# A long convolution's second stage on quarters of TensorE's array, its swapped spectra made there, and the filter's sine arguments on VectorE

## The chip, the cores and the metric

One Trainium2 chip; the program runs on one of its cores. The metric is the device time of one execution in microseconds (us), the median of several. A core has TensorE (matrix products), VectorE, ScalarE, GpSimd, SyncE (which here only issues transfers), and 16 DMA engines that all queues share. TensorE reads SBUF and writes PSUM, which has eight banks of 128 partitions by 512 fp32 values; VectorE and ScalarE read PSUM.

## The reference, cut to what matters

A backbone of two layers over 1024 latent and 256 context tokens of width 1024. Layer 0 is a Hyena mixer (long convolutions with filters made by a small network with sines), layer 1 is latent attention, each followed by a gated feed-forward part. The change touches layer 0's filters and convolutions:

```python
def hyena_filters(L, fw1, fb1, fw2, fb2, fw3, freq):
    ...
    hdn = jnp.sin(freq[0] * (feats @ fw1 + fb1))
    hdn = jnp.sin(freq[1] * (hdn @ fw2 + fb2))
    h = (hdn @ fw3).reshape(L, HY_ORDER, 2, D_MODEL)
    ...
def bidir_long_conv(z, h_fwd, h_bwd, bias):
    L = z.shape[1]
    k = jnp.concatenate([h_fwd, jnp.zeros_like(h_fwd[:1]), h_bwd[1:][::-1]], axis=0)
    kf = jnp.fft.rfft(k.astype(jnp.float32), n=2 * L, axis=0)
    zf = jnp.fft.rfft(z.astype(jnp.float32), n=2 * L, axis=1)
    y = jnp.fft.irfft(zf * kf, n=2 * L, axis=1)[:, :L]
    return (y + z.astype(jnp.float32) * bias).astype(z.dtype)
...
    z = v
    for n, gate in enumerate((x1, x2)):
        z = gate * bidir_long_conv(z, filt[:, n, 0], filt[:, n, 1], fbias[n])
```

## The kernel before

**The filter's sines.** Five products with fw1 and ScalarE (arguments) give 64 x 2560 arguments in turns, in fa. To bring them into half a turn on each side, four elementwise operations run on GpSimd: add MAGIC, subtract it (which rounds), subtract the result, clamp; a semaphore (s_fc) stands between each two. ScalarE takes the sine, TensorE the second layer (128 x 2560), and the four operations run on GpSimd again, after it has issued six loads for VectorE's modulation vectors. Meanwhile VectorE reduces weight tiles against the conditioning (first_mods, 18 tiles, two reductions each, by a custom operation), then scales the eight x tiles and splits them into high and low parts (Hs0), which TensorE's first weight stream waits for tile by tile. SyncE waits for the second reduction (s_fr) before it loads the convolution's constants, and behind them the next weight tiles of that stream.

**The convolution** is a Fourier transform in two stages of matrix products, all in fp32. STEPS is an order of steps written out by hand, and each engine walks it. There are five rounds (it): four for 256 channels each of the latent tokens, and one for the context; in each two convolutions (o). The steps:

- K: filter values (h2 by fw3), decay on VectorE, first stage, eviction to s1 by ScalarE, a store to t2k by GpSimd's queue that regroups the partitions. Six s1 slots.
- Z: signal transposed, first stage in two halves, s1, stores to t2z.
- S: second stage of the filter: t2k by st gives the spectrum, 64 real and 64 imaginary rows, which ScalarE copies to kk[:, 0]. SyncE then copies the two halves of the partitions crosswise into kk[:, 1] by eight DMAs, so that a product with the real spectrum can meet both parts.
- M: eight units. Each has two products of t2z with st (banks 4, 5 in turn), VectorE's multiplication by kk[:, 0] and kk[:, 1] into prod (128 x 1024), and four products with mi and mib (real and crossed part) accumulated in banks 6, 7. ScalarE evicts to one of three w1 slots, GpSimd's queue stores to t2w. TensorE issues unit u's signal products before unit u-1's inverse products.
- B: waits for all t2w stores, then 32 small products with f1i, and VectorE's gating.

The order inside a round is M(it,0), S(it,1), B(it,0), K(it+1,0), Z(it,1), K(it+1,1), M(it,1), Z(it+1,0), S(it+1,0), B(it,1). GpSimd's queue issues the stores in that order, and ScalarE evicts in it.

## Time and profile before

| | before |
|---|---|
| median of 3 runs | 3764.3 us (3762.15 to 3768.49) |
| the profiled execution | 3763.62 us |
| its span, first to last instruction | 3761.9 us |
| TensorE, VectorE, ScalarE, GpSimd busy | 91%, 59%, 35%, 10% |
| mean granted TensorE clock | 0.969 |
| until TensorE's first weight stream runs on | 0 to about 112 us |
| convolution | about 441 to 1162 us |
| a middle round of it | 140 us (841 to 981) |

Times of one instruction come from one profiled execution. In the records a fp32 product appears as two pairs of a weight load (LDWEIGHTS, engine PEld) and a multiply (MATMUL, engine PE), so x2 is one product. A product's duration is modelled and includes its way through the array; what TensorE spends on it is the distance from one start to the next. Idle time of an engine is put down to what ended it.

### The profile page before, as it was taken

To read this page: it belongs to the slowest core of one execution; us is meant where nothing else is said; L and a number is where in the kernel's file an instruction comes from. 1 tells how busy PE (TensorE), PEld (TensorE's weight loads), DVE (VectorE), ACT (ScalarE), POOL (GpSimd) and SP (SyncE) were. 2 spreads that over 40 slices of the span, in tenths; PEclk is the share of its full clock that TensorE was granted. 3 is DMA by queue.
4 is the path that set the end of the run, shared out by engine and by line. 5 is a ranking of instruction groups with operands and counts; after the bars stand their busy time and mean duration, and the time that the engine had idled before them with its cause. 6 is when DMAs were issued, how large, how long until landed. Compare 5 with 4: busy or idle time off the path is not lost.

```text
span 3761.9 us, 44226 instructions
## 1 busy us (share of the span) xinstructions
PE 3412.2 (91%) x16326; PEld 2710.6 (72%) x16326; DVE 2203.0 (59%) x3232; ACT 1325.8 (35%) x2255; POOL 357.7 (10%) x518
## 2 busy tenths in 40 slices
PE   1999988988989989999989988999999979999897
PEld 0788655565677768888868876777777758888685
DVE  8989832332334565545566755555555676666576
ACT  1212233333333353333334543333333353333344
POOL 5111123323330000000000020000000000000000
PEclk9999999999998999999999999999999989999899
DMA  5655799989763132222353431000000223332632
GB/s 192 207 198 201 201 149 149 155 155 150 167 200 135 56 109 84 81 86 90 137 186 98 163 118 45 8 7 7 7 31 0 73 93 123 104 107 87 235 99 89
DMA packets 191373, 430.87 MB, mean 115 GB/s; under 512 B 34560, under 2 KB 61504, under 8 KB 189512
## 3 DMA queue, kind: packets, MB, share of 16 engines
q1 hardware_dynamic: 138984, 291.65, 24.6%
q0 software_dynamic: 51936, 131.27, 16.1%
q10 hardware_dynamic: 288, 5.77, 0.4%
q8 instruction: 103, 1.69, 0.2%
q14 instruction: 62, 0.50, 0.1%
HBM read 262.50 MB, written 81.00 MB: 91 GB/s over the span
## 4 chain that ended last, share of the span: by engine, by line
PE 71%; DVE 12%; DMA 10%; ACT 3%; issue 2%; POOL 1%; SPq 0%; DVEq 0%; ACTq 0%; POOLq 0%
PE ps L602 18%; PE ps L603 18%; PE ps L604 18%; DMA t2z<-s 3%; DMA t2w<-w 3%; PE ps L2375 2%; PE ps L2350 2%; DMA t2k<-s 2%; PE ps L672 1%; DVE mx L2726 1%; PE ps L2333 1%; PE ps L2233 1%; PE ps L2334 1%; PE ps L2319 1%; PE ps L2301 1%
## 5 line engine op out<-in xcount | busy, mean ns | idle before, releaser
L602 PE MATMUL ps<-HB,gsp 128*128 128x512 f32 x1232 | 487.6, 396 | 38.2 <-DVE HB L778 22.0
L603 PE MATMUL ps<-HB,gsp 128*128 128x512 f32 x1232 | 484.1, 393 | 0.0
L604 PE MATMUL ps<-HB,gsp 128*128 128x512 f32 x1232 | 483.0, 392 | 0.0
L1056 DVE TENSOR_TENSOR gsp<-graw,gsp 128x512 fp32r<-128x512 f32 x330 | 226.4, 690 | 262.7 <-ACT gsp L1035 261.9
L1035 ACT ACTIVATE gsp<-graw 128x512 fp32r<-128x512 f32 x330 | 206.8, 628 | 326.2 <-PE ps L604 266.9
L602 PEld LDWEIGHTS ps<-HB,gsp 128*128 128x128 f32 x1232 | 233.9, 190 | 91.8 <-issue 21.5
L602 PE MATMUL ps<-tsp,wdh 128*128 128x512 f32 x616 | 244.1, 396 | 35.6 <-DVE tsp L1313 35.6
L604 PEld LDWEIGHTS ps<-HB,gsp 128*128 128x128 f32 x1232 | 233.6, 190 | 49.9
L603 PEld LDWEIGHTS ps<-HB,gsp 128*128 128x128 f32 x1232 | 233.9, 190 | 46.1 <-issue 1.0
L602 PE MATMUL ps<-Hs,whi 128*128 128x512 f32 (+1 forms) x576 | 206.1, 358 | 47.3 <-DVE Hs L2532 47.3
L603 PE MATMUL ps<-tsp,wdh 128*128 128x512 f32 x616 | 242.2, 393 | 0.0
L604 PE MATMUL ps<-tsp,wdh 128*128 128x512 f32 x616 | 242.2, 393 | 0.0
L603 PE MATMUL ps<-Hs,whi 128*128 128x512 f32 (+1 forms) x576 | 205.5, 357 | 0.0
L604 PE MATMUL ps<-Hs,wlo 128*128 128x512 f32 (+1 forms) x576 | 204.9, 356 | 0.0
L1289 ACT ACTIVATE wdh<-wd 128x512 fp32r<-128x512 f32 x154 | 97.3, 632 | 249.8 <-PE ps L604 235.1
L2645 DVE TENSOR_TENSOR prod<-ps,kk 128x1024 f32<-128x1024 f32 x80 | 97.6, 1224 | 137.6 <-PE ps L2319 136.5
L2059 ACT ACTIVATE s<-ps 128x512 f32<-128x512 f32 x160 | 94.9, 597 | 226.6 <-PE ps L2233 88.5
L1310 DVE TENSOR_TENSOR wdh<-wd,wdh 128x512 fp32r<-128x512 f32 x154 | 106.1, 689 | 115.9 <-ACT wdh L1289 115.2
L1976 POOL DMA_DIRECT2D R<-residual_scratch x6 | 5.3, 891 | 1719.8 <-DMA hidden_scratch<-R 957.7
L2135 ACT ACTIVATE pts<-ps 128x512 fp32r<-128x512 f32 (+1 forms) x192 | 96.4, 524 | 189.8 <-PE ps L2410 188.9
L602 PEld LDWEIGHTS ps<-tsp,wdh 128*128 128x128 f32 x616 | 117.2, 190 | 63.6 <-issue 33.1
L602 PEld LDWEIGHTS ps<-Hs,whi 128*128 128x128 f32 x576 | 109.6, 190 | 66.9 <-issue 46.3
(263 smaller groups left out, 7941.9 us busy)
## 6 DMA issues: line engine op xcount, KB each, us to landing
graw<-in_w_gu SPq DMA_DIRECT2D x176, 256.0 KB, 2.6
mring<-in_mod_w POOLq DMA_DIRECT2D x78, 512.0 KB, 4.3
hidden_scratch<-R SPq DMA_DIRECT2D x154, 256.0 KB, 2.4
traw<-hidden_scratch SPq DMA_DIRECT2D x154, 256.0 KB, 2.6
t2k<-s POOLq DMA_DIRECT2D x80, 256.0 KB, 10.2
t2z<-s POOLq DMA_DIRECT2D x160, 128.0 KB, 8.9
kk<-kk SPq DMA_DIRECT2D x80, 256.0 KB, 7.3
t2w<-w POOLq DMA_DIRECT2D x160, 128.0 KB, 4.9
```

Source lines behind the costliest of these rows:

```text
L602: pe.matmul(o, wh, xh, start=start, stop=False, skip_group_check=onto)
L603: pe.matmul(o, wh, xl, start=False, stop=False, skip_group_check=onto)
L604: return pe.matmul(o, wl, xh, start=False, stop=stop, skip_group_check=onto)
L1035: act.activation(gsp[U % 3][:, 0, :], graw[:, q, W_SLOT[i], :], ACT.Copy).then_inc(w.hi, 1)
L1056: dve.tensor_tensor(gsp[U % 3][:, 1, :], graw[:, q, W_SLOT[i], :], gsp[U % 3][:, 0, :].bitcast(F32), ALU.subtract).then_inc(w.lo, 1)
L1289: act.activation(wdh[v % 3][:, 0, :], wd[W_SLOT[i]][:, kt, :], ACT.Copy).then_inc(w.hi, 1)
L1310: dve.tensor_tensor(wdh[v % 3][:, 1, :], wd[W_SLOT[i]][:, kt, :], wdh[v % 3][:, 0, :].bitcast(F32), ALU.subtract).then_inc(w.lo, 1)
L2059: act.activation(s1[b % 6][:], bank(BANK_B[b % 2]), ACT.Copy).then_inc(s_be, 1)
L2135: act.activation(dst, src, ACT.Copy).then_inc(s_ma, 1)
L2350: mm = pe.matmul(ps[:, BANK_A[au % 2], 64 * k:64 * k + 64], t2w[:, at:at + P], f1i[:, which, :], start=True, stop=True)
L2375: mm = pe.matmul(bank(use.bank, n), whq[:, k, o:o + P], cq[:, k, t0:t0 + n], start=(k == 0), stop=(k == 2))
L2645: dve.tensor_tensor(prod[zi % 2][:], bank(BANK_C[(n["c"] + u) % 2]).unsqueeze(1).to_broadcast([P, 2, 512]), kk[:, :, 512 * u:512 * (u + 1) ...
```

## The change

1. **Quarters.** st and mi are cut into 64x64 blocks. A full 128x128 product becomes four products (QUARTERS), with row half r of the input and output half c, each on its own quarter of the array; their results go to two banks (one for each r in S and the signal part of M). Input halves and output halves hold different frequencies now: of each pair of frequency groups one lies in the upper and one in the lower partitions, with real and imaginary parts in the two banks.
2. **Swaps.** st2 holds the blocks in the order real, imaginary, imaginary, real, so M's signal part makes spectrum and swapped spectrum by products (v = 0, 1). kk[:, o] holds one unswapped copy per convolution, and SyncE's eight DMAs of each S step are gone. VectorE multiplies both banks by kk, read twice.
3. **Inverse.** Each product with mi or mib is four quarters, with the input halves c and output halves r; results of two units share two banks.
4. **PSUM.** Signal results use banks 4, 5 and 0, 1 in turn (A's), outputs 6, 7 and 2, 3 (B's), so M waits for A and B to be emptied, and the next K or Z for the outputs (EMPTIED_BEFORE).
5. **Sine arguments.** The eight operations move from GpSimd to VectorE: the first four behind the first six modulation tiles, the other four behind the last high-low split of x.

```diff
+    half = [slice(32 * r, 32 * r + 32) for r in range(2)]
+    st2, mi2 = np.zeros((P, NB, 4, 32)), np.zeros((2, 2, 32, 2, NB, 2, 64))
...
@@ sync
-                elif kind == "S":
-                    for q in range(4):
-                        sp.wait_ge(s_ke, n["k"] + 2 * q + 2)
-                        cols_ = slice(1024 * q, 1024 * (q + 1))
-                        sp.dma_start(kk[0:64, 1, cols_], kk[64:P, 0, cols_]).then_inc(s_sw[q], 16)
-                        sp.dma_start(kk[64:P, 1, cols_], kk[0:64, 0, cols_]).then_inc(s_sw[q], 16)
@@ gpsimd
-            for layer, rows in enumerate((64, P)):
-                pool.wait_ge(s_fa, NFC * (layer + 1))
...
-                if layer == 0:
-                    mod_load(3)
+            mod_load(3)
@@ scalar, step S
-                    for u in range(8):
+                    for u in range(4):
                         act.wait_ge(s_kf, n["k"] + u + 1)
-                        act.activation(kk[:, 0, 512 * u:512 * u + 512], bank(BANK_C[(n["c"] + u) % 2]), ACT.Copy
-                                       ).then_inc(s_ke, 1)
+                        act.activation(kk[:, o, 1024 * u:1024 * u + 1024].rearrange("p (a r c) -> p r a c", a=2, r=2),
+                                       pair(SETS_S[u % 2]).rearrange("p r (a c) -> p r a c", a=2), ACT.Copy).then_inc(s_ke, 1)
@@ tensor, step S
+                            for r, c in QUARTERS:
+                                e = 4 * u + 2 * h + c
+                                mm = pe.matmul(ps[rows64(c), SETS_S[u % 2] + r, CW * h:CW * (h + 1)],
+                                               st[rows64(r), const_at(it, e), 0:64],
+                                               t2k[rows64(r), 512 * e + CW * o:512 * e + CW * (o + 1)], start=True, stop=True)
@@ tensor, step M
+                        if u == 1:
+                            pe.wait_ge(s_ae, n["A"])
...
+                            for v in range(2):
+                                for r, c in QUARTERS:
+                                    e = 2 * u + c
+                                    mm = pe.matmul(ps[rows64(c), SETS_C[u % 2] + r, CW * v:CW * (v + 1)],
+                                                   st[rows64(r), const_at(it, e), 64 * v:64 * v + 64],
+                                                   t2z[rows64(r), CW * e:CW * (e + 1)], start=True, stop=True)
...
+                            y = u - 1
+                            pe.wait_ge(s_pr, n["z"] + y + 1)
+                            if y == 2:
+                                pe.wait_ge(s_be, n["B"])
+                            if y in (4, 6):
+                                pe.wait_ge(s_de, n["d"] + y - 2)
+                            for v, m_ in enumerate((mi, mib)):
+                                for r, c in QUARTERS:
+                                    mm = pe.matmul(ps[rows64(r), SETS_D[y // 2 % 2] + c, CW * (y % 2):CW * (y % 2 + 1)],
+                                                   m_[rows64(c), const_at(it, 2 * y + c), 64 * r:64 * r + 64],
+                                                   prod[y % 2][rows64(c), r, CW * v:CW * (v + 1)], start=v == 0, stop=v == 1)
...
@@ vector
+            def reduce_arguments(layer, rows):
+                dve.wait_ge(s_fa, NFC * (layer + 1))
+                x, u = fa[0:rows, :], fu[0:rows, :]
+                dve.tensor_scalar(u, x, MAGIC, None, ALU.add).then_inc(s_fc, 1)
...
+            first_mods(range(6))
+            reduce_arguments(0, 64)
+            first_mods(range(6, 18))
...
+            reduce_arguments(1, P)
@@ vector, step M
-                        dve.tensor_tensor(prod[zi % 2][:],
-                                          bank(BANK_C[(n["c"] + u) % 2]).unsqueeze(1).to_broadcast([P, 2, 512]),
-                                          kk[:, :, 512 * u:512 * (u + 1)], ALU.mult).then_inc(s_pr, 1)
+                        dve.tensor_tensor(prod[zi % 2][:].rearrange("p r (v c) -> p r v c", v=2),
+                                          pair(SETS_C[u % 2]).rearrange("p r (v c) -> p r v c", v=2),
+                                          kk[:, o, 512 * u:512 * (u + 1)].rearrange("p (r c) -> p r c", r=2).unsqueeze(2)
+                                          .to_broadcast([P, 2, 2, CW]), ALU.mult).then_inc(s_pr, 1)
```

TensorE's row in step M, two units of the steady part, before (a row is one product; "waits" names the semaphores; ps is PSUM):

```order
L2319 MATMUL ps<-t2z,st 128x256 [waits products_ready]
L2319 MATMUL ps<-t2z,st 128x256
L2333 MATMUL ps<-prod,mi 128x256 [waits inverse_emptied,products_ready]
L2334 MATMUL ps<-prod,mib 128x256
L2333 MATMUL ps<-prod,mi 128x256
L2334 MATMUL ps<-prod,mib 128x256
L2319 MATMUL ps<-t2z,st 128x256 [waits products_ready]
L2319 MATMUL ps<-t2z,st 128x256
```

And now (x7 and x4 count products in a row):

```order
L2330 MATMUL ps<-t2z,st 64x256 [waits products_ready]
L2330 MATMUL ps<-t2z,st 64x256 x7
L2346 MATMUL ps<-prod,mi 64x256 [waits inverse_emptied,products_ready]
L2346 MATMUL ps<-prod,mi 64x256 x3
L2346 MATMUL ps<-prod,mib 64x256 x4
```

Six full products of a unit have become sixteen quarter products: eight with st behind one another, then four with mi and four with mib.

VectorE's row at the start, behind the first six modulation tiles (macc and modv), now:

```order
L2514 ISA macc 128x1
L2520 TENSOR_TENSOR modv<-macc,modb 128x12 [waits mod_w_used]
L2537 TENSOR_SCALAR fu<-fa 64x2560 [waits filter_arguments_out_or_even_products_used]
L2539 TENSOR_SCALAR fu<-fu 64x2560 [waits filter_reduction_step]
L2541 TENSOR_TENSOR fa<-fa,fu 64x2560 [waits filter_reduction_step]
L2543 TENSOR_SCALAR fa<-fa 64x2560 [waits filter_reduction_step]
L2514 ISA junk,macc<-mring,cond 128x1024 [waits mod_w_used,weight_tile_loaded0,mod_stored]
L2514 ISA macc 128x1
```

Four elementwise operations (L2537 to L2543) stand between the sixth tile's sum and the seventh tile, where the two followed each other directly. Before, GpSimd had them (with six loads between the two fours):

```order
L1926 TENSOR_SCALAR fu<-fa 64x2560 [waits filter_arguments_out]
L1927 TENSOR_SCALAR fu<-fu 64x2560 [waits filter_reduction_step]
L1928 TENSOR_TENSOR fa<-fa,fu 64x2560 [waits filter_reduction_step]
L1932 TENSOR_SCALAR fa<-fa 64x2560 [waits filter_reduction_step]
L1918 DMA mring<-in_mod_w 128x1024 [waits mod_w_used] x6
L1926 TENSOR_SCALAR fu<-fa 128x2560 [waits filter_arguments_out]
L1927 TENSOR_SCALAR fu<-fu 128x2560 [waits filter_reduction_step]
L1928 TENSOR_TENSOR fa<-fa,fu 128x2560 [waits filter_reduction_step]
L1932 TENSOR_SCALAR fa<-fa 128x2560 [waits filter_reduction_step]
```

GpSimd's queue now goes straight to its twelve loads. The second four stand on VectorE behind the last split of x (L2562), ahead of the weight stream's next low part (L573):

```order
L2562 TENSOR_TENSOR Hs<-xr,Hs 128x1280 [waits x_tile_high] x2
L2537 TENSOR_SCALAR fu<-fa 128x2560 [waits filter_arguments_out_or_even_products_used]
L2539 TENSOR_SCALAR fu<-fu 128x2560 [waits filter_reduction_step]
L2541 TENSOR_TENSOR fa<-fa,fu 128x2560 [waits filter_reduction_step]
L2543 TENSOR_SCALAR fa<-fa 128x2560 [waits filter_reduction_step]
L573 TENSOR_TENSOR wlo<-wraw,whi 128x512 [waits ring_w_high]
```

So that low part, and what TensorE needs of it, comes after them; the row before had it directly behind the splits.

## Rows read from the trace of the kernel before

**Rows 1.** The page: span, and busy time of each engine.

```profile
span 3761.9 us, 44226 instructions
...
PE 3412.2 (91%) x16326; PEld 2710.6 (72%) x16326; DVE 2203.0 (59%) x3232; ACT 1325.8 (35%) x2255; POOL 357.7 (10%) x518
```

**Rows 2.** A round: us; busy PE, PEld, DVE, ACT, POOL; clock, DMA share, GB/s.

```profile
841.00:981.00 140.00, 120.71 (x509) 85.46 (x508) 41.33 (x48) 43.06 (x79) 46.42 (x79) 0.96 0.94 153
```

**Rows 3.** DMA, 841 to 981 us: queues (packets, MB, share); issues (KB, us to landing).

```profile
q0 software_dynamic: 7274, 12.53, 66.5%
q1 hardware_dynamic: 2786, 8.79, 27.2%
...
kk<-kk SPq DMA_DIRECT2D x16, 256.0 KB, 9.0
```

**Rows 4.** Chain of waits, 838 to 985 us: start, us, what was waited for.

```profile
919.71 12.60 DMA t2z<-s
...
943.71 11.06 DMA t2w<-w
```

**Rows 5.** Waits of TensorE, 841 to 981 us: in total, times, longest.

```profile
PE ps L2333 <- ACT w L2102: 8.3, 2, 5.2
```

**Rows 6.** Timeline of TensorE's products in step M: start, us, line, tiles.

```profile
941.17 0.59 PE L2333 MATMUL ps<-prod,mi 128*128 128x256 f32 x2
941.60 0.59 PE L2334 MATMUL ps<-prod,mib 128*128 128x256 f32 x2
942.04 1.03 PE L2319 MATMUL ps<-t2z,st 128*128 128x256 f32 x4
```

**Rows 7.** Timeline of loads (PEld) and VectorE in the same stretch.

```profile
941.39 0.41 PEld L2334 LDWEIGHTS ps<-prod,mib 128*128 128x128 f32 x2
...
943.10 1.22 DVE L2645 TENSOR_TENSOR prod<-ps,kk 128x1024 f32<-128x1024 f32 x1 [1.36 <-PE ps L2319]
```

**Rows 8.** Timeline of the inverse transform, at full and at half granted clock.

```profile
966.26 7.25 PE L2350 MATMUL ps<-f1i,t2w 128*128 128x64 f32 x64
973.36 2.07 PE L2264 MATMUL ps<-fw,h 128*128 128x512 f32 x4
...
1148.60 13.89 PE L2350 MATMUL ps<-f1i,t2w 128*128 128x64 f32 x64 [3.50 <-issue]
```

**Rows 9.** Timeline of VectorE and GpSimd, 19 to 44 us.

```profile
19.07 1.22 DVE L2497 CUSTOM_DVE_ANT_0 mring<-mring,cond 128x1024 f32<-128x1024 f32 x1
...
20.21 6.82 DVE L2497 CUSTOM_DVE_ANT_0 junk<-mring,cond 128x1024 f32<-128x1024 f32 x1
...
40.24 3.32 DVE L2497 CUSTOM_DVE_ANT_0 mring<-mring,cond 128x1024 f32<-128x1024 f32 x1
...
19.87 6.96 POOL L1926 TENSOR_SCALAR fu<-fa 64x2560 f32<-64x2560 f32 x1 [19.29 <-ACT fa L2019]
...
39.31 3.17 POOL L1932 TENSOR_SCALAR fa<-fa 64x2560 f32<-64x2560 f32 x1
```

**Rows 10.** Timeline of VectorE and GpSimd, 72 to 113 us.

```profile
75.17 4.39 DVE L557 TENSOR_TENSOR wlo<-wraw,whi 128x512 fp32r<-128x512 f32 x2 [3.03 <-ACT whi L552]
79.48 15.85 DVE L2528 TENSOR_SCALAR xr<-xr,onep,modv 128x1024 f32<-128x1024 f32 x4
95.25 1.48 DVE L2532 TENSOR_TENSOR Hs<-xr,Hs 128x1280 fp32r<-128x1280 f32 x1
96.65 1.12 DVE L2528 TENSOR_SCALAR xr<-xr,onep,modv 128x1024 f32<-128x1024 f32 x2
...
112.77 0.68 DVE L557 TENSOR_TENSOR wlo<-wraw,whi 128x512 fp32r<-128x512 f32 x1
...
72.62 6.66 POOL L1926 TENSOR_SCALAR fu<-fa 128x2560 f32<-128x2560 f32 x1
...
92.14 2.32 POOL L1932 TENSOR_SCALAR fa<-fa 128x2560 f32<-128x2560 f32 x1
```

**Rows 11.** Instruction group of VectorE, 0 to 130 us: count, busy us, mean ns.

```profile
L2555 DVE TENSOR_SCALAR uo<-ubuf,vecs 128x1282 f32<-128x1282 f32 x1 | 0.9, 939 | 0.0
```

More of the change, by code:

```diff
@@ L112, in dft_constants @@
                 st[:, g, 0, col], st[:, g, 1, col] = vre, vim
-    return f1, f1i, st, mi
+    half = [slice(32 * r, 32 * r + 32) for r in range(2)]
+    st2, mi2 = np.zeros((P, NB, 4, 32)), np.zeros((2, 2, 32, 2, NB, 2, 64))
+    for r in range(2):
+        rows = slice(64 * r, 64 * r + 64)
+        for i, part in enumerate((0, 1, 1, 0)):
+            st2[rows, :, i] = st[rows, :, part, half[r]]
+        for part in range(2):
+            mi2[:, part, :, :, :, r] = mi.reshape(2, 64, 2, NB, P)[part, half[r], :, :, rows]
+    return f1, f1i, st2, mi2.reshape(P, 2, NB, P)
 def filter_constants(L):
@@ L468, in build @@
         s_sum = sem("channel_sum_added")
-        s_wr = [sem(f"spectrum_swapped_or_mixer_weight_loaded{i}") for i in range(4)]
+        s_wr = [sem(f"mixer_weight_loaded{i}") for i in range(4)]
         s_wr += [sem(f"filter_or_mixer_weights_loaded{i}") for i in range(2)]
         s_sw, s_jl = s_wr[0:4], s_wr[4:6]
-        WR_AT = (64 * NIT,) * 4 + (24 * (NCH + 4),) * 2
+        WR_AT = (0,) * 4 + (24 * (NCH + 4),) * 2
         s_yhi, s_ylo = sem("mixer_output_high"), sem("mixer_output_split")
@@ L485, in build @@
         s_fp = sem("filter_psum_full")
-        s_fa = sem("filter_arguments_out")
+        s_fa = sem("filter_arguments_out_or_even_products_used")
+        s_dm, DM_AT = s_fa, 2 * NFC
         s_fc = sem("filter_reduction_step")
@@ L542, in bank, with pair, rows64 @@
             return ps[:, i, 0:n]
+        def pair(i):
+            return ps[:, i:i + 2, :]
+        def rows64(i):
+            return slice(64 * i, 64 * i + 64)
         def split_hi(act, sm, t, h, C, first):
@@ L2101, in _ @@
                             act.wait_ge(s_w1o[d % 3], 32 * (d // 3))
-                        act.activation(w1[d % 3][:], bank(BANK_D[d % 2]), ACT.Copy).then_inc(s_de, 1)
+                        act.activation(w1[d % 3][:], bank(SETS_D[u // 2 % 2] + u % 2), ACT.Copy).then_inc(s_de, 1)
                         if tail and u == 5:
@@ L2296, in _ @@
                     sent(pe, B_END["K", it, 1])
-                    for u in range(8):
-                        bk = spectrum_bank(n["c"] + u)
-                        for h in range(2):
-                            e = 2 * u + h
-                            mm = pe.matmul(ps[:, bk, CW * h:CW * (h + 1)], st[:, const_at(it, e), :],
-                                           t2k[:, 512 * e + CW * o:512 * e + CW * (o + 1)], start=True, stop=True)
+                    for u in range(4):
+                        if u == 1 and n["d"]:
+                            pe.wait_ge(s_de, n["d"] - 2)
+                        if u >= 2:
+                            pe.wait_ge(s_ke, n["k"] + u - 1)
+                        for h in range(2):
+                            for r, c in QUARTERS:
[3 more added lines that the diff above has]
+                                               t2k[rows64(r), 512 * e + CW * o:512 * e + CW * (o + 1)], start=True, stop=True)
                         mm.then_inc(s_kf, 1)
@@ L2314, in _ @@
                     for u in range(9):
-                        if u < 8:
-                            bk = spectrum_bank(n["c"] + u)
-                            for h in range(2):
-                                e = 2 * u + h
-                                mm = pe.matmul(ps[:, bk, CW * h:CW * (h + 1)], st[:, const_at(it, e), :],
-                                               t2z[:, CW * e:CW * (e + 1)], start=True, stop=True)
+                        if u == 0:
+                            pe.wait_ge(s_ke, 4 * (2 * it + o + 1))
+                        if u == 1:
+                            pe.wait_ge(s_ae, n["A"])
+                        if 2 <= u < 8:
+                            pe.wait_ge(s_pr, n["z"] + u - 1)
+                        if u < 8:
+                            for v in range(2):
[4 more added lines that the diff above has]
+                                                   t2z[rows64(r), CW * e:CW * (e + 1)], start=True, stop=True)
                             mm.then_inc(s_zf, 1)
@@ L2325, in _ @@
                         if u >= 1:
[L2326 to L2336 removed]
+                            y = u - 1
[9 more added lines that the diff above has]
+                                                   prod[y % 2][rows64(c), r, CW * v:CW * (v + 1)], start=v == 0, stop=v == 1)
+                                    if v == 1 and r == 1 and y % 2 == 1:
+                                        mm.then_inc(s_df, 1)
+                            if y % 2 == 0:
+                                mm.then_inc(s_dm, 1)
                 else:
                     if it == NCH and o == 1:
+                        pe.wait_ge(s_de, N_Z)
                         mix_pe(pe, 0, 0)
```

73 lines of the change are left out of this document (30 added, 43 removed).

## The prediction

> **What bounds the kernel now.** I read the page first: TensorE is busy 91% of a span of 3761.9 us and VectorE 59% [rows 1]. The profiled execution took 3763.6 us, so 1.7 us lie around the span; the sum below is made against it, and it stands 0.7 under the median of the three runs, 3764.3. Two stretches hold the change: 0 to 112 us, before TensorE streams, and the convolution, 441 to about 1162 us. I cut the convolution into its five rounds. A middle round takes 140 us; TensorE is busy 120.7 of them and the 16 DMA engines 94% of the time [rows 2]. So two resources are nearly full together, and neither can be relieved alone. By queue, GpSimd's (q0: stores of first-stage results and of w1) takes 66.5%, SyncE's (q1) 27.2%. The swaps kk<-kk are 16 x 256 KB = 4.2 MB of q1's 8.79 MB; by bytes that is 13.0% of 140 us, **18.2 us of all DMA engines** [rows 3]. The chain of waits goes through landings of 11 to 13 us, and the list of waits has TensorE stop 8.3 us in this round for ScalarE's eviction to w1, itself held by its slot's landing [rows 4, 5]. Last the instructions one by one: a 128x128 by 256-column product is two load-and-multiply pairs and takes 0.43 us start to start (941.17, 941.60, 942.04); a unit of step M is six of them, 2.59 us [rows 6].
>
> **Part 1, arithmetic of the second stage.** Before, M has 8 units x 6 products x 0.432 = 20.7 us and S has 16 x 0.432 = 6.9 us [rows 6]. After, four 64x64 products form a batch that does the full array's work: M has 8 x 4 batches, S has 8. No row shows two quarters at once, so the price of a batch is the unknown. From below: four streams side by side, 0.43 us, one product's time. The loads set another end. In the inverse transform a pair with 64 moving columns still takes 7.1/64 = 0.111 us, so 128 weight columns cost up to 0.111 us and 64 some 0.055 (an estimate by halving); that this is the array's clock and not the sequencer shows in the same 64 pairs at half the granted clock, 13.9 us [rows 8]. A batch has eight pairs: 8 x 0.055 = 0.44 us. From above: four products one after the other, 1.73 us. I take 0.45, nearest to the row of one full product, because the full array already loads under a running product: the loads of the row at 941.39 lie inside the product row that begins at 941.17 [rows 6, 7]. Then M is 14.4 us (-6.3), S 3.6 (-3.3), and a round of two each gives TensorE back **19.2 us**.
>
> **Part 2, the swaps go.** 18.2 us of DMA time a round, as above. So both full resources are relieved by nearly the same, 140 - 19.2 and 140 - 18.2, and the smaller counts. The remaining bound is DMA: stores of w1 are 256 KB a unit, and q0 spent 66.5% of 140 us on 12.5 MB, 1.95 us per 256 KB [rows 3], over TensorE's new 1.8 us a unit. Some DMA idle time grows, because step B needs all w1 stores landed and the next store comes only after it. I take **17 us a round, 5 x 17 = 85 us**.
>
> **Part 3, VectorE and ScalarE in the second stage.** The product still writes 128x1024 and now also reads 1024 from two PSUM banks; the row is 1.22 us [rows 7]. Between the end of a signal batch and the need of its product TensorE has 1.8 us of other batches, over 1.22 plus some 0.2 of hand-over, so it stays hidden by 0.4 us; if it took over 1.6 us, M would be paced by VectorE. ScalarE takes 4 x 1024 columns in S instead of 8 x 512: a little less. New waits: M's unit 1 waits for bank A emptied, its output 2 for bank B emptied, the next signal step for all outputs emptied. Behind these stand only TensorE's own products, and ScalarE works through s1 before w1 in order already, so the same landing is waited for. I price them at 0, at most 1 us each, 5 a round, kept for the range.
>
> **Part 4, the sine arguments.** While GpSimd runs its four operations from 19.87 to 42.5 us, VectorE's reductions of 1.15 us each stretch: four take 20.21 to 43.56, 23.3 us instead of 4.6, **18.7 lost** [rows 9]. The second time, with GpSimd from 72.6 to 94.5, two weight splits and four scalings take 75.17 to 95.3, 20.2 us; undisturbed they are 2 x 0.68 and 2 x 1.12, 3.6, and I allow 0.2 for ScalarE's first high part, so **16.4 lost** [rows 10]. After the change VectorE runs the eight operations itself: by its 1282-column row at 0.94 us, 2560 columns are 1.9 us, and the two-input one, by 1.48 us for 1280 columns, 3.0 [rows 10, 11]: 3 x 1.9 + 3.0 = 8.7 at most, 6.9 if the scalings run at the rate of the faster 1024-column ones inside the 1.12 us of two [rows 10]. I take 7.5 each. The first sits on the path: 18.7 - 7.5 = 11.2 gained. Nothing waits for it longer: its arguments are out at 19.8 and six tiles end at about 25. The second follows the last high-low split, when TensorE has started: behind it on VectorE stands the next weight split, behind it on SyncE (filter_reduced) the constants and the next weight loads. TensorE has part of tile 0 left then, so between 0 and 7.5 us show, plus some for loads; I take 5. Gain 16.4 - 5 = 11.4. Together **23 us**, between 15 and 30.
>
> **Sum.** 3763.6 - 85 - 23 = 3655.6, **3656 us**.
>
> **Rivals.** *A, the DMA time isn't given back in full.* A landing that is waited for takes 11 to 13 us [rows 4], far over the time of its bytes, and the waits are in series: B waits for w1's stores, M for t2z's. If the shorter M only moves TensorE's idle time ahead of B, the round gives 8 us and not 17: 3763.6 - 40 - 23 = **3701**. For it: DMA is already idle in short pauses in B. Against it: shorter queues make landings quicker.
> *B, half the quarters at once.* Each fp32 quarter product is two pairs on the same quarter, and its second multiply can't start before its first ends, 0.216 us. If multiplies start strictly in program order, only the second pass of one quarter runs beside the first of the next: 4 x 0.216 = 0.86 us a batch [rows 6]. M is 27.6 (+6.9), S 6.9 (0); +13.8 a round, less 8.3 of w1 waits and 1 to 2 of others: +4, so 3763.6 + 20 - 23 = **3761**, no change. For it: every row has multiplies in program order; nothing shows two at once.
> The Trainium skill speaks for B: TensorE: Matmul & The Clock Gate, Part 3, says that multiplies start and end in program order and that a load overlaps a running multiply only when its row group differs. By the first, 3761 as worked out; the trace can't contradict it. On the second the trace disagrees for whole-array products, whose loads lie under the multiply before them [rows 7]; by it a batch would be near rival C's. The same section reports a sixteen-fold packing at 10.6 times the speed, which speaks for my 0.45, for products of one pass.
> *C, slower: loads not hidden.* If a quarter's load can't lie under the product of its own or its neighbour's row group, each pass costs 0.216 + 0.055 and only the two row groups run side by side: 4 x 0.271 = 1.08 us a batch. M is 34.6 (+13.9), S 8.6 (+1.7): +31 a round, less 9 of waits = +22; 3763.6 + 110 - 23 = **3851**. Without any overlap (1.73 us) 80 batches a round cost 138 us for 55: about **4100**. The point where the change turns to loss is 0.86 us a batch: 80 x 0.86 = 69 is 55 + 9 of waits + 5 from part 4.
>
> **Chances.** Forecast 44%, A 16%, B 20%, C 20%. A difference of 0.2% (7.5 us) is what a measurement of this kernel can tell. Forecast and A are faster; of B two fifths lie under 3756, a quarter is within 0.2%, the rest slower; C is slower. That is 0.68 faster, 0.05 same, 0.27 slower. The forecast's own range is 3630 to 3685 (part 4 from 15 to 30, a round from 13 to 20). The range takes in A and B and leaves out most of C: 3630 to 3820.
>
> **What would show it.** Right: quarter products whose starts in a batch average about 0.055 us per pair; M at about 1.8 us a unit; DMA share still over 85% in a round of 120 to 125 us; no kk<-kk; VectorE's reductions at 1.15 us through 20 to 45 us, first product of the weight stream near 70 us instead of 97. Wrong: pairs 0.11 us apart (B), 0.13 and more (C), or a DMA share well under 80% with a round over 130 us (A). VectorE's product over 1.6 us, or TensorE waiting over 5 us for the weight split after the second reduction, would fault parts 3 and 4.

## The result, and the profile after

The changed kernel takes **3744.2 us** (median of 9 runs, 3730.1 to 3756.3) against 3764.3 in the same comparison (9 runs, 3757.0 to 3774.0): ratio **0.9939, 95% interval 0.9920 to 0.9958**. That is 20 us faster by the medians (23 by the ratio), inside the range and with the sign forecast, but a fifth of the 108 us forecast. The page, span and busy times [rows 1]:

```profile
span 3741.8 us, 47892 instructions
...
PE 3368.0 (90%) x18246; PEld 2622.9 (70%) x18246; DVE 2181.8 (58%) x3240; ACT 1316.5 (35%) x2215; POOL 314.1 (8%) x510
```

A round of the convolution, and four short stretches of it or near it (windows; us; busy PE, PEld, DVE, ACT, POOL; granted clock, DMA share, GB/s):

```profile
821.00:962.00 141.00, 115.00 (x890) 69.16 (x889) 41.22 (x48) 40.50 (x69) 45.97 (x79) 0.83 0.76 122
924.00:928.00 4.00, 2.06 (x44) 1.20 (x37) 2.45 (x2) 0.60 (x1) 0.00 (x0) 1.00 1.03 105
943.00:957.00 14.00, 13.60 (x64) 13.63 (x65) 2.07 (x3) 1.26 (x3) 0.00 (x0) 0.50 0.00 0
989.00:997.00 8.00, 5.46 (x9) 2.38 (x10) 2.75 (x4) 3.61 (x8) 1.70 (x3) 0.79 1.08 121
999.00:1003.00 4.00, 3.96 (x23) 1.45 (x22) 1.66 (x3) 2.20 (x5) 1.59 (x3) 1.00 0.93 341
```

The round is still 141 us. TensorE has 115.0 us of work in it instead of 120.7 and the DMA engines stand at 0.76 instead of 0.94 [rows 2]: both resources were relieved and nothing came out at the end. The third row is an inverse transform: TensorE at clock 0.50 (1.2 GHz), DMA at 0. The last two lie just behind the round: the fourth has stores to t2z in flight, the fifth the first stores of the fifth round, the context's. The last column needs a second look: at a full DMA share the second row moves 105 GB/s and the fourth 121, the last 341 at 0.93. More on that below. The queues of the round (packets, MB, share) and one group of issues (KB each, us to landing):

```profile
q0 software_dynamic: 7337, 12.56, 64.1%
q1 hardware_dynamic: 1453, 4.44, 11.6%
...
t2w<-w POOLq DMA_DIRECT2D x32, 128.0 KB, 5.9
```

q1's share fell by 15.6 points (27.2% in [rows 3]), which is the swaps; q0's fell by 2.4. **Quarters**: timeline of step M, where x8 is a batch of four products of two pairs:

```profile
864.22 1.04 PE L2330 MATMUL ps<-t2z,st 64*64 64x256 f32 x16
865.08 0.61 PE L2346 MATMUL ps<-prod,mi 64*64 64x256 f32 x8
865.51 0.61 PE L2346 MATMUL ps<-prod,mib 64*64 64x256 f32 x8
865.94 1.04 PE L2330 MATMUL ps<-t2z,st 64*64 64x256 f32 x16
```

A batch takes 0.43 us (865.08 to 865.51), a unit 1.73 us, for 2.59 before [rows 6]. VectorE's product is hidden as before [rows 7]:

```profile
865.33 1.23 DVE L2676 TENSOR_TENSOR prod<-ps,kk 128x1024 f32<-128x1024 f32 x1 [0.50 <-PE ps L2330]
```

**Start**: VectorE's reductions (first and second), and TensorE's first product of the stream, now and before:

```profile
24.28 1.48 DVE L2537 TENSOR_SCALAR fu<-fa 64x2560 f32<-64x2560 f32 x1
25.79 1.48 DVE L2539 TENSOR_SCALAR fu<-fu 64x2560 f32<-64x2560 f32 x1
27.31 2.82 DVE L2541 TENSOR_TENSOR fa<-fa,fu 64x2560 f32<-64x2560 f32 x1
30.16 1.48 DVE L2543 TENSOR_SCALAR fa<-fa 64x2560 f32<-64x2560 f32 x1
...
88.71 1.49 DVE L2537 TENSOR_SCALAR fu<-fa 128x2560 f32<-128x2560 f32 x1
...
94.62 1.49 DVE L2543 TENSOR_SCALAR fa<-fa 128x2560 f32<-128x2560 f32 x1
```

```profile
72.82 0.77 PE L618 MATMUL ps<-Hs,whi 128*128 128x512 f32 x1 [31.56 <-DVE Hs L2562]
```

```profile
96.87 0.77 PE L602 MATMUL ps<-Hs,whi 128*128 128x512 f32 x1 [44.78 <-DVE Hs L2532]
```

Each reduction takes 7.4 us from its start to its end (24.28 to 31.64), none of VectorE's other work stretches any longer [rows 9, 10], and the stream's first product starts 24.0 us earlier. Of that, 16 us are left where the convolution's first S starts, at 478.5 us for 494.6 before.

**Where the round's time is.** Chain of waits (start, us, what), then TensorE's and ScalarE's waits over the round (total, times, longest):

```profile
836.27 12.25 DMA t2z<-s
...
867.63 12.04 DMA t2w<-w
...
882.39 6.77 DMA t2w<-w
...
920.93 9.27 DMA t2w<-w
...
931.76 5.28 DMA t2w<-w
```

```profile
ACT w L2103 <- DMA t2w<-w: 29.0, 10, 9.5
...
PE ps L2249 <- ACT w L2103: 4.1, 1, 4.1
...
PE ps L2346 <- ACT w L2103: 3.8, 2, 1.9
PE ps L2305 <- ACT kk L2090: 3.7, 2, 3.1
...
PE ps L2305 <- ACT w L2103: 2.8, 1, 2.8
```

The long landings stand as in [rows 4], up to 12 us, and in each M a second one of w1's follows the first (6.77 behind 12.04, 5.28 behind 9.27). M waited twice for w1 before, 8.3 us in all [rows 5]; now there are waits of Z (L2249, 4.1 us), M (L2346, 3.8 us), and S (L2305) for ScalarE, which itself waits 29.0 us for w1's landings. ScalarE's evictions to w1 in M of order 0, then two inverse transforms, order-1 B and order-0 B, which is the step behind M and S:

```profile
918.29 1.09 ACT L2103 ACTIVATE w<-ps 128x512 f32<-128x512 f32 x2 [11.48 <-PE ps L2346]
...
927.23 0.60 ACT L2103 ACTIVATE w<-ps 128x512 f32<-128x512 f32 x1 [4.89 <-DMA t2w<-w]
930.28 0.60 ACT L2103 ACTIVATE w<-ps 128x512 f32<-128x512 f32 x1 [2.46 <-DMA t2w<-w]
932.95 0.60 ACT L2103 ACTIVATE w<-ps 128x512 f32<-128x512 f32 x1 [2.07 <-DMA t2w<-w]
```

```profile
905.65 7.36 PE L2367 MATMUL ps<-f1i,t2w 128*128 128x64 f32 x64
...
943.40 13.88 PE L2367 MATMUL ps<-f1i,t2w 128*128 128x64 f32 x64 [1.02 <-issue]
```

The evictions come 2 to 5.5 us apart, where TensorE offers one per 1.73; S waits behind them, and order-0 B takes 13.88 us instead of 7.25 [rows 8]. Before it TensorE was busy 4.8 of the 10 us from 928 to 938, at a granted clock of 0.77; in the 5.4 us after them the clock was 0.50, the lower of its two levels (1.2 and 2.4 GHz).

### The profile page after: what moved, and what is told of

The parts are those of the page before. It is cut to its first block, busy times and chain, and to the rows that moved or that the text cites. A ratio compares the mean times of both kernels' runs of the same rounds, so it can differ in the third digit from the quotient of the medians.

```text
span 3741.8 us, 47892 instructions
## 1 busy us (share of the span) xinstructions
PE 3368.0 (90%) x18246; PEld 2622.9 (70%) x18246; DVE 2181.8 (58%) x3240; ACT 1316.5 (35%) x2215; POOL 314.1 (8%) x510
## 4 chain that ended last, share of the span: by engine, by line
PE 71%; DVE 12%; DMA 11%; ACT 3%; issue 3%; POOL 1%; SPq 0%; DVEq 0%; ACTq 0%
PE ps L618 18%; PE ps L620 18%; PE ps L619 18%; DMA t2w<-w 4%; PE ps L2367 3%; PE ps L2392 3%; DMA t2z<-s 2%; DMA t2k<-s 2%; PE ps L688 1%; PE ps L2240 1%; DVE mx L2758 1%; PE ps L2264 1%; PE ps L2249 1%; PE ps L2427 1%; PE ps L2330 1%
```

## The experiments

A *round* in the table is the distance between the starts of the first and the last order-0 B, over 4, from one profiled execution. The ratio is to the kernel before on the same chip. The control's (e13) profiled execution took 3756.7 us, 16 over its median, so its round is too long by some 3 us; e17's lay 12 under its median.

| run | us | ratio, 95% interval | round |
|---|---|---|---|
| before | 3764.3 | | 136.8 |
| changed | 3744.2 | 0.9939 (0.9920-0.9958) | 135.3 |
| e1 sine arguments alone | 3745.5 | 0.9941 (0.9921-0.9960) | 136.2 |
| e3 before, no swaps | 3757.3 | 0.9965 (0.9949-0.9982) | 134.8 |
| e13 changed, kk single (control) | 3741.0 | 0.9928 (0.9911-0.9944) | 138.2 |
| e4 changed, swaps back | 3786.3 | 1.0039 (1.0024-1.0055) | 146.0 |
| e5 changed, 8 slots of w1 | 3762.4 | 0.9977 (0.9968-0.9987) | 139.0 |
| e9 changed, fillers | 3736.9 | 0.9911 (0.9890-0.9931) | 136.1 |
| e6 changed, K first | 3715.3 | 0.9859 (0.9840-0.9877) | 124.6 |
| e7 changed, K first, 8 slots | 3699.9 | 0.9825 (0.9801-0.9849) | 121.7 |
| e8 before, K first | 3758.2 | 0.9968 (0.9950-0.9985) | 132.8 |
| e10 changed, t2w spread | 3662.2 | 0.9719 (0.9703-0.9735) | 117.8 |
| e11 changed, all spread | 3599.2 | 0.9553 (0.9537-0.9569) | 109.1 |
| e12 before, all spread | 3672.1 | 0.9750 (0.9733-0.9766) | 120.0 |
| e14 changed, reordered stores | 3647.0 | 0.9670 (0.9624-0.9716) | 119.4 |
| e15 before, reordered stores | 3694.1 | 0.9811 (0.9768-0.9853) | 123.4 |
| e17 changed, reordered, K first | 3638.4 | 0.9658 (0.9617-0.9700) | 109.9 |
| **e16 the same with 8 slots** | **3603.9** | **0.9566 (0.9524-0.9609)** | 103.9 |
| e18 before, reordered, K first | 3693.7 | 0.9808 (0.9790-0.9826) | 121.5 |
| e19 changed, reordered, swaps back | 3691.8 | 0.9811 (0.9780-0.9842) | 127.9 |

**e1: the sine arguments alone.** Four operations per layer from GpSimd to VectorE, as in the change; nothing else.

> The kernel before with one part of the change alone: the sine arguments reduced on VectorE, convolution as before. In the changed kernel the convolution starts some 19 us earlier and lasts as long as before (about 718 us). Theory 1 (the whole gain of the change is this part): 3764 - 20 = 3744 us, the same as the changed kernel. Rival (the convolution gave something back as well, or the start is worth less): 3755 us or more.

24 us faster than before (22 by the ratio), the changed kernel's own time. The whole gain is part 4; the convolution's part is nothing that can be told: the two intervals leave some 10 us either way, 2 a round.

**e3: no swaps in the kernel before.** The swapped half is left out, so the result is not the full one.

```diff
-  sp.dma_start(kk[0:64, 1, cols_], kk[64:P, 0, cols_]) ... (both, x4)
-  kk[:, :, 512 * u:512 * (u + 1)]
+  kk[:, 0, 512 * u:512 * (u + 1)].unsqueeze(1).to_broadcast([P, 2, 512])
```

> The kernel before without the swap copies: nothing is copied, and the product reads the unswapped half of kk twice (the swapped spectrum is left out of the result). Everything else is as before. Theory 1 (the copies lay in stretches in which the DMA engines had nothing else to do, around step B, so their 18 us a round were free): 3764 us, at most 10 less. Rival, the forecast's own reading (both TensorE and DMA are full, each of their waits shortens with the queues): at least part of the 8.3 us of w1 waits a round goes, 40 us or more off: 3725 us or less.

12 us, 2.5 a round: between the two, a little over the theory's 10.

**e4: the swaps back in the changed kernel**, and **e13**, its control.

```diff
-  act.activation(kk[:, o, 1024 * u: ...
+  act.activation(kk[:, 0, 1024 * u: ...          (e4, e13, e5)
+  sp.dma_start(kk[0:64, 1, cols_], kk[64:P, 0, cols_]) ...   (e4 alone)
```

> The changed kernel with the sixteen 256 KB swap copies of a round put back on the DMA queue: they go into the half of kk that nothing reads (kk holds one order's spectra at a time, where the changed kernel holds two), and the product waits for them as before. The result is the full one. Forecast's reading (a round is paced by the DMA engines' time): 5 x 17 us more, about 3830 us. Theory 1 (a round is a chain of landings that are waited for, and the copies fall into its pauses): 3744 to 3755 us.

> The changed kernel with kk holding the spectra of one order at a time, and nothing else: the control for the runs with the swaps put back (3786 us) and with 8 slots (3762 us), which both contain this. Its ScalarE waits for the last product of a step M before it empties the first banks of S. If that costs nothing: 3744 us, and the swaps cost 42 us when they are put back. If it costs 10 us or more, as much of both differences belongs to it.

The control is level with the changed kernel, so the swaps cost 45 us here (42 by the ratios), 9 a round: neither 17 nor nothing. e4's order-0 B waits for a landing and runs at half clock:

```profile
828.05 13.91 PE L2373 MATMUL ps<-f1i,t2w 128*128 128x64 f32 x64 [3.41 <-DMA t2w<-w]
```

The control's does too (13.91 us, at 811.2), so the clock isn't the difference; S in front of it waits 5.6 us for ScalarE's evictions to w1, 2.0 in the control. e4 shows one thing more. It is the kernel before with the quarters and the sine arguments, and with the swaps kept, and it is 41 us slower than e1, which has the sine arguments alone (ratios 1.0039 and 0.9941). So as long as the swaps stay, the quarters, with the waits that come with them, make this kernel slower.

**e5: 8 slots of w1.**

```diff
-  w1 = [... for i in range(3)]
+  w1 = [... for i in range(3)] + [kk[:, 1, 512 * i:512 * (i + 1)] for i in range(5)]
```

> The changed kernel with 8 slots of w1 instead of 3 (five of them in the half of kk that comes free when kk holds one order at a time); the result is the full one. Theory 1a (with 3 slots and a landing of 5.6 us each, ScalarE's eviction to w1 follows at one unit per 2 to 2.9 us, and S and B come behind it): the eight evictions follow M at 1.8 us, S before B takes 7 us instead of 12.7, B starts 4 to 8 us earlier in each half round: 3744 - 25 to - 60, about 3700 us. Theory 1b (stores leave at 1.95 us per unit whatever the slots, so the last landing before B comes when it came): within 10 us of 3744. Theory 2 (the half clock in step B is what eats the gain): also within 10 us, with step B still at 12 to 14 us.

Theory 1a fell, with a loss of 18 us (21 against the control, which has kk for one order too, as e7 and e16 have) that 1b did not expect either. S (4.3 us) no longer waits, but B does, and the stores leave at 105 GB/s with the DMA engines full (window between them):

```profile
672.02 13.89 PE L2368 MATMUL ps<-f1i,t2w 128*128 128x64 f32 x64 [12.89 <-DMA t2w<-kk]
```

```profile
656.00:666.00 10.00, 2.77 (x48) 1.26 (x40) 0.00 (x0) 4.71 (x7) 2.29 (x4) 0.88 1.07 105
```

**e9: fillers.** 13 products whose result nobody reads, in S of order 1.

```diff
+  for i in range(n_ if o == 1 else 0):
+      pe.matmul(bank(0, CW), st[:, 0, :], t2z[:, 0:CW], start=True, stop=True)
```

> The changed kernel with 13 filler products (128x128 by 256 columns, 5.6 us of TensorE at full clock) in step S of order 1, at the places where TensorE waits for the evictions: 5, 5 and 3 ahead of B. Nobody reads what they make; the result is the full one. Theory 2 (half clock in B, 11.7 to 13.9 us instead of 7.3, is what ate the gain): B back at 7.3 us, 5 to 6 us a round: about 3718 us. Theory 1 (stores and landings set the round): B at full clock ends earlier only where its start isn't set back, and K's stores follow at once: half of it, 3730 us. If the clock stays at half in spite of them: 3744 us or a little more.

B of order 0 ran at full clock in the last three rounds of five and not in the first two; in the changed kernel it did so in the first round alone:

```profile
671.20 13.41 PE L2374 MATMUL ps<-f1i,t2w 128*128 128x64 f32 x64 [2.01 <-DMA t2w<-w]
...
814.98 7.36 PE L2374 MATMUL ps<-f1i,t2w 128*128 128x64 f32 x64 [0.78 <-DMA t2w<-w]
```

The gain over the changed kernel is 7 us with overlapping intervals, and the round isn't shorter (136.1). The clock takes 4 to 6.6 us from B (11.7 to 13.9 us for 7.3), but not the 17.

**e6, e7, e8: K of the next round ahead of B of order 0.**

```diff
-  STEPS += [("M", it, 0), ("S", it, 1), ("B", it, 0)]
-  STEPS += [("K", it + 1, 0)] if more else []
-  STEPS += [("Z", it, 1)]
+  STEPS += [("M", it, 0), ("S", it, 1)]
+  STEPS += [("K", it + 1, 0)] if more else []
+  STEPS += [("B", it, 0), ("Z", it, 1)]
```

> The changed kernel with one step moved: the first half of the next round's filter stage (K) is done before the inverse transform (B) of order 0 instead of behind it, so TensorE has 14 us of products while the last stores of w1 land, and the DMA engines have the stores of K to send while B runs. In the changed kernel they stand at 14% and 6% of their time in the two 10 us stretches of that B, which itself takes 11.7 to 13.9 us at half clock. Theory 1 (TensorE's idle time and DMA's idle time alternate there): B at 7.3 us, its wait gone, 10 to 18 us a round, four rounds: 3744 - 40 to - 70, about 3685 us. Rival (the DMA engines' work of a round in all sets it): 3735 us or more.

> The changed kernel with K moved ahead of B of order 0 and with 8 slots of w1. With three slots ScalarE holds evictions of s1 (K's) behind those of w1, which wait for landings; with K directly behind M this could matter more. If slots matter there: faster than K moved alone by 10 us or more. If only the rate of the stores matters (as the run with 8 slots alone, which lost 18 us against the changed kernel, says): the same or slower than K moved alone.

> The kernel before with the same step moved (K of the next round ahead of B of order 0), nothing else. There TensorE is busy 120.7 us of a round of 140 and step B runs at full clock in most rounds. Theory 1: little to win, since the wait ahead of B is 1 us and TensorE's own work stands close to the round: 3764 - 0 to - 20. If it gains as much as the changed kernel does by the same move, then the smaller TensorE work of the change buys nothing even without the wait.

29 us, 44 us and 11 us, the last against the kernel before. In the signal rounds B runs at full clock and waits for nothing (`804.34 7.25` in e6's timeline), but the rounds stay over 120 us. Slots, a loss alone, gain 15 us here. e6 fell short of its theory's 40 us, so the rival holds in part: something paces the round besides the order.

**e10, e11, e12: stores spread over 32 partitions.** In the fifth round, the context's, stores to t2k, t2z and t2w were quick. Their destination is the difference: `t[first:P:nb]` is 32 partitions there and 8 in the signal rounds. These runs use the context's pattern everywhere (e10 for t2w alone), so the layout is wrong and the values are not the reference's.

```diff
+  if it < NCH:
+      it, first, at = NCH, first % 4, width * (first // 4)
```

> The changed kernel with one thing different: in the four signal rounds each w1 store (128 KB, by 1 KB pieces) goes to 32 partitions of t2w instead of 8, as it does in the fifth, context, round. Same bytes, same number of stores; where the values land is not what the inverse transform needs, so the output is not the reference's. In the traces GpSimd's 4 KB packets take about 185 ns in the context round's M (1055 to 1070 us) and 500 to 630 ns in the M steps of the signal rounds. Theory 3 (the eight destination partitions make the stores slow, and the landing of the last one sets when B starts): packets at about 185 ns, w1 waits and the wait ahead of B gone, B at full clock, M+S+B of order 0 from 44 us to about 29, order 1 likewise some 5 to 8 us: about 3744 - 4 x 18 = 3670 us. Theory 2 (clock alone): unchanged. If something else of the context round makes its packets quick: unchanged, 3744 us.

> The changed kernel with all three kinds of stores (t2k, t2z, t2w) spread over 32 destination partitions in the signal rounds; the output is not the reference's. Theory 3: DMA no longer paces anything, a round falls to TensorE's own work and the chain of B, about 110 us: 3744 - 4 x 30 = 3624 us. Beside the next run it shows what TensorE's smaller work is worth when the stores do not set the round.

> The kernel before with the same spread of all three kinds of stores (the output is not the reference's). Its TensorE work of a round is 120 us and hardly shrinks, so theory 3 expects a round of 125 us: 3764 - 4 x 15 = 3704 us, that is some 60 us more than the changed kernel's arithmetic gains under the same spread once the start's 20 us are taken off, near the 19 us a round of my forecast. Rival (TensorE's smaller work buys nothing whatever the stores do): the difference between this and the changed kernel's run stays at the start's 20 us.

82, 145 and 92 us, the last two more than expected. In e10's M w1's stores land in 2.2 us instead of 5.9, and take 0.45 of the DMA engines' time for 153 GB/s, 340 for a full share, where the changed kernel has 105 at 1.03 (window and issues):

```profile
750.00:757.00 7.00, 6.53 (x124) 4.60 (x120) 3.67 (x3) 2.53 (x6) 4.45 (x9) 1.00 0.45 153
```

```profile
t2w<-w POOLq DMA_DIRECT2D x9, 128.0 KB, 2.2
```

These runs change a second thing: the same bytes go in fewer packets (q0 sends 4352 in a round of e11, 7424 in the changed kernel), so they don't show alone that the number of partitions is the cause. With the stores quick the change shows: the rounds are 109.1 us in e11 and 120.0 in e12, 11 us for the 18 that M and S save (B of order 0 still falls to half clock in two of e11's rounds). How much of the 11 is TensorE's work and how much the swaps that only e12 has, no run shows. A pair of order-0 Bs of each:

```profile
818.41 7.33 PE L2369 MATMUL ps<-f1i,t2w 128*128 128x64 f32 x64 [0.91 <-DMA t2w<-w]
...
929.75 7.36 PE L2369 MATMUL ps<-f1i,t2w 128*128 128x64 f32 x64
```

```profile
754.35 7.36 PE L2352 MATMUL ps<-f1i,t2w 128*128 128x64 f32 x64 [0.83 <-DMA t2w<-w]
...
872.33 7.25 PE L2352 MATMUL ps<-f1i,t2w 128*128 128x64 f32 x64
```

**e14 to e17: the same bytes to the same places, in another order.**

```diff
+  if it < NCH:                              # K: filter units
+      e = 4 * (e % 4) + e // 4
-  n2 = 2 * u + m2 + 8 * h                   # Z
+  n2 = u + 4 * m2 + 8 * h
-  e = 2 * u + c                             # S, M and w1's stores
+  e = 2 * (0, 2, 4, 6, 1, 3, 5, 7)[u] + c
```

> The changed kernel with the stores left as they are (each to the 8 partitions that it needs) and only their order changed in the signal rounds, so that stores that follow each other go to partitions of different groups: filter units in the order 0, 4, 8, 12, 1, ..., the signal's pairs u and u+4 instead of 2u and 2u+1, and the second stage's units in the order 0, 2, 4, 6, 1, 3, 5, 7. The result is the full one. By the Trainium skill (SBUF - State Buffer, Door 1: the DMA port swizzle) partitions g, g+16, ..., g+112 reach 4 of 16 ports, and which 4 depends on g/4 rounded down; its figure for 4 ports is 104 GB/s. The rows: 103 to 118 GB/s while such stores run, 372 GB/s for those over 32 partitions. Theory 3 (stores one behind another to the same group are what is slow): with neighbours in different groups most of what the spread runs gained comes back, 3744 - 100 = 3640 us. Rival (each store alone is slow on its 8 partitions and the engines run them one at a time): no gain, 3735 to 3750 us.

> The kernel before with the same reordering of stores and units and nothing else; the result is the full one. If the order alone relieves the stores: 3764 - 70 = 3694 us, and the difference to the changed kernel with it is then the start's 20 us and some 30 to 50 us of TensorE time and swaps. If not: 3755 to 3770 us.

> The changed kernel with the reordered stores, K of the next round ahead of B of order 0, and 8 slots of w1. The result is the full one. If the stores are quick through their order, K ahead of B gives less than its 29 us, since the wait ahead of B is short by then: 3620 to 3640 us. If the order does nothing: 3700 us, as the run without it.

> As the run before it in this list, with the three slots of w1 that the changed kernel has. If slots matter only where stores are slow: the same time as with 8 slots within 10 us.

Theory 3 held, with the full result: 97 us from the order of stores and units alone in the changed kernel, 70 in the one before. Packets and bytes are the same, and q0's packets take 45.7% of a round of 123 us in e14 (626 to 749 us), 56 us of all DMA engines for 12.63 MB; the changed kernel's took 64.1% of 141 us, 90 us for 12.56 MB. A stretch with the engines full moves 179 GB/s in e14 and 196 in e16:

```profile
790.00:800.00 10.00, 5.14 (x9) 1.97 (x8) 2.07 (x3) 2.98 (x6) 2.49 (x5) 0.83 0.98 179
```

```profile
645.00:655.00 10.00, 7.46 (x18) 3.34 (x18) 3.46 (x5) 5.91 (x12) 3.02 (x6) 1.00 0.98 196
```

K first adds 9 us with three slots, which the intervals don't tell from nothing. The slots' expectation missed: with K first they are worth 35 us (e17 to e16), and so e16 came out under its 3620 to 3640. **e16, 3603.9 us, beats both kernels.** Its order-0 Bs, 105.4 us apart, and those of e18:

```profile
621.69 7.25 PE L2374 MATMUL ps<-f1i,t2w 128*128 128x64 f32 x64
...
727.06 7.26 PE L2374 MATMUL ps<-f1i,t2w 128*128 128x64 f32 x64
```

```profile
665.40 7.25 PE L2356 MATMUL ps<-f1i,t2w 128*128 128x64 f32 x64
...
791.67 7.25 PE L2356 MATMUL ps<-f1i,t2w 128*128 128x64 f32 x64
```

**e18, e19: what the change is worth then.**

> The kernel before with both remedies that its memory allows (stores reordered over the partition groups, K of the next round ahead of B of order 0; the 8 slots of w1 have no room there, because the swapped spectra take it). The result is the full one. With the reordered stores alone its rounds were 124 to 126 us, with TensorE at work nearly all the time and B at full clock. If TensorE bounds it then, K first gives nothing: 3685 to 3695 us, and against the changed kernel with both remedies and 8 slots (3604 us) the change is worth about 85 us in such surroundings, 20 of it from the start and some 13 a round. If it gains as the changed kernel did (9 us with three slots, 43 with eight): 3680 us or less.

> The changed kernel with the reordered stores and the swap copies put back (as in the run of that name, with kk for one order at a time). Without the reordering they cost 3786 - 741 - 3000 = 45 us against the control (3741), 9 a round, for 17 forecast. If they cost because the DMA engines' time is short: less now that the stores take less of it, 3647 + 10 to + 25. If they cost because their own landing is waited for between S and M whatever else the engines do: 3647 + 45 = 3692 us.

e18 is level with e15: K first gives nothing in the kernel before, where TensorE is busy 119 of 126 us of a round (e15, 645 to 771 us) and so bounds it. The change is worth 90 us against e16, 55 with three slots in both (e17), of which 24 are e1's; the 8 slots belong to the change only in so far as the swapped spectra leave them no room in the kernel before. In e19 the swaps still cost 45 us, so it isn't short DMA time as such. M to B of order 0 takes 29.6 us instead of 24.3 in e14, with S waiting for ScalarE's eviction to w1, and B is at half clock in all five rounds, in e14 in two of five. Its order-0 Bs take 21 us more in all, which can be up to half of the 45 us. S and the B behind it, and the next round's B:

```profile
750.05 1.99 PE L2317 MATMUL ps<-t2k,st 64*64 64x256 f32 x16 [3.72 <-ACT w L2115]
...
759.59 13.92 PE L2379 MATMUL ps<-f1i,t2w 128*128 128x64 f32 x64 [1.40 <-DMA t2w<-w]
...
889.50 13.89 PE L2379 MATMUL ps<-f1i,t2w 128*128 128x64 f32 x64 [4.60 <-issue]
```

e19 is also level with e15 (3691.8 and 3694.1 us, both 0.9811), the kernel before with the same order of stores. Swaps are in both, so quarters and sine arguments together give nothing there that the intervals (some 20 us either way) can tell, though the second are worth 24 us alone.

## Why the prediction was right or wrong

**Part 1 was right.** 0.43 us a batch for 0.45, 1.73 us a unit; S and M without waits are 18 us a round shorter (e11's M 15.5 to 16.0 and S 4.3 to 6.6, e12's M 21.7 and S 7.4 to 9.6), for 19.2 forecast. Rivals B and C are out. The Trainium skill's rule that multiplies start and end in program order (TensorE: Matmul & The Clock Gate, Part 3) would have given 0.86 as rival B applied it; the timeline has eight pairs in 0.43 us, so by duration quarters ran side by side.

**Part 4 was right.** Two reductions of 7.4 us for 7.5, 24 us (e1) for 23.

**Part 3 mis-sized its waits.** "Behind these stand only TensorE's own products" was wrong: Z's first product now waits for ScalarE to empty w1's banks, 4.1 us here, and from Z's first product to the first of S it took 15.0 us (884.1 to 899.1) where it took 7.5 (906.9 to 914.5 before); its products ran slower too, the first ones in 3.75 us for 1.98. In e16, with 8 slots and quick stores, Z takes 7.7 us, so the wait hangs on w1's landings.

**Part 2 was wrong, and it is the step that failed**: "So both full resources are relieved by nearly the same ... I take 17 us a round". Three things lay in it, and a fourth that the sum didn't have.

First, a DMA share of 94% was read as one full resource that any byte relieves. It isn't one: from M's start to order-0 B the changed kernel took 30.5 us (912.9 to 943.4), and 33.7 before (932.6 to 966.3). In it lie 5.4 us until the first eviction, 19.4 for ScalarE's eight evictions to w1 (918.3 to 937.7) and 5.7 until B starts. w1's 2.1 MB at 105 GB/s would be 20 us, which fits the 19.4; but a load of 1 MB (gbuf) goes in the same stretch, and from 928 to 938 us the DMA share is 0.64 at 104 GB/s, so three slots and the rate hold the evictions together. Shortening M by 6 us and S by 3 gained 3, and the clock took it back: B at 13.88.

Second, "1.95 us per 256 KB" was q0's mean over the round, with K's stores and idle stretches in it. At the 105 GB/s of M it is 2.5 us. That is over TensorE's new 1.73 a unit, and almost what TensorE took before (2.59). The row to read was GB/s beside the DMA share, stretch by stretch.

Third, why they are slow. The rows show 105 to 121 GB/s for stores whose destination is partitions g, g+16, ..., g+112, 341 for the fifth round's K, and 179 to 196 when neighbours have g in different fours (e14, e16). The Trainium skill states a rule that fits (SBUF — State Buffer, Door 1: the DMA port swizzle): bits 2 to 4 and bit 6 of the partition number choose one of 16 ports. Partitions g + 16j reach four, chosen by g/4; that page's figure for four ports is 104 GB/s, and the trace has 105 to 121. That the ports are the cause is not shown by itself; that the order is, e14 and e15 show. The prediction weighed TensorE's rules and not that one. Rival A named the symptom, "the shorter M only moves TensorE's idle time ahead of B", at 16% and with 8 us a round, and its sign came (a DMA share of 0.76 with a round of 141 us); the truth was 0 to 1.5.

Fourth, the sum had no term for the granted clock. In four rounds of five B of order 0 took 11.7 to 13.9 us, at a granted clock of 0.50 to 0.59; in the kernel before in none, 7.3 or 7.4 us each. The prediction had both rows of that clock [rows 8] and priced it at nothing.

Once the stores are relieved the change gains, by the profiled rounds 4.0 us a round (e15 to e14), 11.6 with K first too (e18 to e17) and 17.6 with 8 slots as well (e18 to e16); by the medians, less the start's 24 us, 4.6, 6.2 and 13.1. That the last is near the 17 forecast is luck: the forecast had neither the slots nor the order in it, and it took the round as the smaller of two reliefs. By e4 and e19 the quarters gained nothing while the swaps stayed, with slow stores or quicker ones, and by e3 the swaps alone gained 12 us. What stays open: why swaps cost 45 us in the changed kernel in both orders but 12 in the one before (in e19 at most 21 of it is the slower B; why the clock falls with them is open too); why 8 slots alone lose 18 us; and how much of e16's gain over e17 is w1's slots in M and how much in Z.

## What to carry to other kernels

Two nearly full resources are not one sum: ask for each stretch what ends it, and relieve that first; here a change worth 0 to 1.5 us a round became worth 4 to 5 once the order of stores was changed, and 13 to 18 with the order of steps and 8 slots too. Test the parts of a change apart as well: with the swaps kept, the quarters made this kernel slower. Read a DMA share together with its GB/s: a full share at a third of the best rate of the same trace is a pattern problem, and neighbours in a queue should go to partitions of different groups. An engine made faster on a chain of landings turns idle, and here its granted clock then fell for the step behind.

## What the runs showed of the hardware

- Stores of 128 KB to 8 partitions 16 apart move 105 to 121 GB/s at a DMA share of 1.03 to 1.08 (changed kernel, e5); with neighbouring stores in different fours, 179 to 196 at 0.98 (e14, e16); to 32 partitions 4 apart, in fewer packets, 341 at 0.93 (256 KB stores, fifth round) and 153 at 0.45 (e10).
- More such stores in flight did not help: 105 GB/s with 3 slots (924 to 928 us) and with 8 (e5).
- Fp32 products of 64x64 by 256 columns on four quarters: 0.43 us for four, one full product's time.
- TensorE behind a stretch in which it was busy 4.8 of 10 us runs the same 64 pairs in 13.9 us instead of 7.3; over the rounds 11.7 to 13.9. With fillers in the gaps B had full clock in three rounds of five (e9), without them in one.
- VectorE's elementwise operation on 2560 columns takes 1.48 us for one input and 2.82 for two, with 64 or 128 partitions alike.
